# Loads of w_mod's units: from the sync engine's queue to ScalarE's own, one unit per round, two steps ahead of use

## The chip, the cores and the metric

The kernel runs on one core of a Trainium2 chip (trn2). The metric is the device time of one execution in microseconds (us), with all inputs in the chip's memory at the start and the output there at the end. The engines that matter here are PE (TensorE, matmuls), DVE (VectorE), ACT (ScalarE) and SP (the sync engine, which here only issues transfers). Each works through its own list in order; they meet through semaphores. 16 DMA engines move the data.

## What is computed

Two blocks on 256 tokens of width 2048, all in float32. The first has two layers of latent attention, a gated convolution, attention to a memory of 256 tokens, a gate and an output projection. The second is one layer with a Fourier mixer and an MLP of width 8192; both are modulated by six vectors of 2048 values that come from one vector `c` and a weight `w_mod` of 2048 x 12288:

```
# first block, for each of 2 layers
h = rmsnorm(x, pre_norm_g[l]);  z = h @ w_in[l]
q_lat, kv_lat, k_pe, gb, gc, xin, q_mem, gate = split_cols(z)
q = rmsnorm(q_lat) @ w_uq[l];  kv = rmsnorm(kv_lat) @ w_ukv[l]     # rope on parts of q and on k_pe
a_out = softmax(q k^T) v;  c_out = gb * conv(gc * xin)
m_out = memory attention of q_mem with rmsnorm(mem) @ w_mk[l], @ w_mv[l]
x = x + rmsnorm((concat(a_out, c_out, m_out) * silu(gate)) @ w_o[l], post_norm_g[l])
# second block
sh1, sc1, g1, sh2, sc2, g2 = split(silu(c) @ w_mod + b_mod, 6)
x = x + g1 * rms_norm(fft_mix(rms_norm(x) * (1 + sc1) + sh1) @ fnet_w_out)
x = x + g2 * rms_norm(relu(modulated(x, sh2, sc2) @ w_mlp_in)^2 @ w_mlp_out)
```

## The kernel before

**Steps.** The work is cut into 576 steps. Two steps use one weight unit of up to 1 MB (2048 columns on 128 partitions). A step's weights are split into a rounded high part (`whi`, made by ACT, line 383) and the rest (`wlo`, made by DVE in place of the raw weight, line 390), and PE multiplies both parts with a likewise split input (line 394). A full step keeps PE busy for about 2.72 us. Steps 0 to 143 are layer 1 of the first block, 144 to 287 layer 2, 288 to 319 the Fourier mixer's projection, 320 to 575 the MLP. In a layer the groups of steps are: memory keys and values, latents, `gc`, `uq`, `ukv` (steps of half the width), `xin`, `gb`, `qmem`, `gate`, `wo` (the last 32).

**Rings.** Four raw units (`raw`), four high halves (`whi`). In round s ACT and DVE first do the split for step s + 3 (`split_hi`, `split_lo`), then whatever else belongs to the round: softmax, the gate (xhalf, tanh, `Y`), squares, the reading of an accumulator that has ended. SP issues a weight unit when PE is through with the unit four before it (`load_unit`, line 357; semaphore `half_used`).

**w_mod.** The product silu(c) @ w_mod isn't done by PE but by DVE: `w_mod` is cut into 12 chunks of 1024 columns, each of 16 units of 128 rows (512 KB, one row of 4 KB per partition), 192 in all. DVE scales a unit and adds it to `modacc` (lines 1019 and 1022), in rounds that a planner picks (`MOD_AT`, two of them at most one step apart where DVE has room, none in rounds called `HEAVY`). After the 16th unit of a chunk PE adds up `modacc` over the partitions with 8 one-column matmuls (`mod_sums`), at the head of a step at least two after the last unit (`MOD_SUM`: steps 49, 82, 105, 126, 166, 204, 232, 255, 277, 308, 359, 421), and waits for that unit there (`mod_used`). The units of the fourth chunk end in step 124, its sum is in step 126; the eighth ends in step 253 and is summed in 255; the ninth ends in 275 and is summed in 277.

**The loads of these units.** They have three buffers (`modw`, `MRING`). Before, SP issues them between the weights: after the weight unit u come the mod units, if any, of steps 2u - 4 and 2u - 3 (`load_mods`, `MOD_LEAD` = 4; line 505), each behind a wait that DVE has used the unit three before it. ACT issues only a few transfers of its own, among them `rowb`, 1 MB that is spread from a row in memory to all partitions (line 692), and SP also the memory's tiles for the next layer (`memr`, line 508, behind a wait) and the gains.

Of the kernel before, what the change touches and what calls it, by code (L numbers as in the profile page):

```python
# [13 lines left out]
P = 128  # L14
# [3 lines left out]
KT = D // P  # L18
# [46 lines left out]
FN_H = DEPTH * LH  # L65
# [74 lines left out]

MCH = MODCOLS // 1024
MRING = 3
MOD_LEAD = 4
M3_BUSY = {q + PV_LAG for q in QK_AT}

HEAVY = ({21, 24, 26, 28, 30, 31, 32, 33, 39, 40, 41, 42, 44, 46, 48, 49, 51, 52, 54, 55, 56, 63} | set(range(64, 69)) | {72, 77, 84}
# [64 lines left out]
def build_program(nc, x, memt, positions, small, w_in, w_uq, w_ukv, w_mk, w_mv, w_o, post_g,  # L211
# [3 lines left out]
    with ctx:  # L215
# [277 lines left out]
        @block.sync  # L493
        def _(sp):
            mem_w = (w_mk, w_mv)

            def load_mods(step):

                for s in (step, step + 1):
                    if s in MOD_AT:  # L500
                        j = MOD_AT[s]
                        if j >= MRING:
                            sp.wait_ge(mod_used, j - MRING + 1)
                        k, c = j % KT, j // KT
                        sp.dma_start(modw[j % MRING][:, :], w_mod[k * P:(k + 1) * P, 1024 * c:1024 * (c + 1)]).then_inc(mod_in[j % MRING], 16)

            def load_mem(b):
                sp.dma_start(memr[:, b % 2, :, :], memt[4 * b:4 * b + 4].rearrange("k p n -> p k n")).then_inc(memr_in[b % 2], 16)

            def load_memx(b):  # L510
                sp.dma_start(memx[:, 4 * b:4 * b + 4, :], memt[4 * b:4 * b + 4].rearrange("k p n -> p k n")).then_inc(mem_in[b], 16)

            for i in range(2):
                sp.dma_start(memx[:, 2 * i:2 * i + 2, :], memt[2 * i:2 * i + 2].rearrange("k p n -> p k n")).then_inc((mem_first, mem_in[0])[i], 16)
                sp.dma_start(raw[0][:, 1024 * i:1024 * (i + 1)].rearrange("p (k n) -> p k n", k=2),
                             weight_rows(w_mk[0], 2 * i, 2, 0, 512)).then_inc((first_in, raw_in[0])[i], 16)
            for l in range(DEPTH):
                src = {"qlat": (w_in[l], C_Q), "kvlat": (w_in[l], C_KV), "gc": (w_in[l], C_GC), "uq": (w_uq[l], 0),
                       "ukv": (w_ukv[l], 0), "xin": (w_in[l], C_XIN), "gb": (w_in[l], C_GB), "qmem": (w_in[l], C_QM),
                       "gate": (w_in[l], C_GATE), "wo": (w_o[l], 0)}  # L520
                for g, (name, kind, width, units, nk) in enumerate(GROUPS):
                    for i in range(units):
                        at_unit = UNIT_AT[g] + i
                        u = l * LU + at_unit
                        if kind == "MEM":
                            if u:
                                load_unit(sp, u, slot(u, nk, width), weight_rows(mem_w[i % 2][l], i // 2 * nk, nk, 0, width))
                            if l == 0 and 1 <= i < 4:
                                load_memx(i)
                            if l == 0 and i == 3:  # L530
                                sp.dma_start(ident[:, :], consts).then_inc(ident_in, 16)
                                sp.dma_start(cv[:, 0:KT], cvec).then_inc(c_in, 16)
                                sp.dma_start(ropev[:, :], rope_c).then_inc(rope_in, 16)
                                sp.dma_start(pos[:, :], positions.partition_broadcast(P)).then_inc(rope_in, 16)
                                sp.dma_start(modT[:, :], bmod).then_inc(vec_in, 16)
                                sp.dma_start(ngs[:, :], ng2).then_inc(vec_in, 16)
                            if l == 0 and i == 4:
                                sp.dma_start(X[:, :, :], x.rearrange("(t p) d -> p t d", p=P)).then_inc(x_in, 16)
                            if l and at_unit in (2, 4):
                                b = at_unit // 2 + 1  # L540
                                sp.wait_ge(mem_lo, l * KT + 4 * (b - 1))
                                load_mem(b)
                        else:
                            w, c0 = src[name]
                            if name == "gate":
                                of = g - G_OF[name]
                                c0 = C_GATE + (2 * GATE_PART[of // 2] + of % 2 - of) * width
                            load_unit(sp, u, slot(u, nk, width),
                                      weight_rows(w, i * nk, nk, c0 + (g - G_OF[name]) * width, width))
                        load_mods(2 * u - MOD_LEAD)  # L550
                    if g == G_OF["wo"] - 1:

                        sp.wait_ge(o_out, l * NH + NH)
                        sp.wait_ge(conv_step, 12 * l + 12)
                        if l + 1 < DEPTH:
                            sp.dma_start(gs[:, :], small[l + 1]).then_inc(small_in, 16)
                        else:
                            sp.dma_start(cs[:, :, :], dft.rearrange("(t p) n -> p t n", p=P)).then_inc(dft_in, 16)
                        sp.dma_start(post[:, :], post_g[l:l + 1, :].partition_broadcast(P)).then_inc(post_in, 16)
                    if g == G_OF["wo"] + 1 and l + 1 < DEPTH:  # L560
                        sp.wait_ge(y_lo, l * 4 + 4)
                        load_mem(0)
                        load_mem(1)
            for i in range(4):
                u = FN_H // 2 + i
                load_unit(sp, u, slot(u, 4, 512), weight_rows(w_fnet, 4 * i, 4, 0, 512))
                load_mods(2 * u - MOD_LEAD)
            for n in range(1, 4):
                for i in range(4):
                    u = FN_H // 2 + 4 * n + i  # L570
                    load_unit(sp, u, slot(u, 4, 512), weight_rows(w_fnet, 4 * i, 4, 512 * n, 512))
                    load_mods(2 * u - MOD_LEAD)
            for q in range(4):
                for n in range(8):
                    for i in range(4):
                        u = ML_H // 2 + 32 * q + 4 * n + i
                        w = w_mlp_in[:, D * q:D * (q + 1)] if n < 4 else w_mlp_out[D * q:D * (q + 1), :]
                        load_unit(sp, u, slot(u, 4, 512), weight_rows(w, 4 * i, 4, 512 * (n % 4), 512))
                        load_mods(2 * u - MOD_LEAD)
            for i in range(2 * MT):  # L580
                sp.wait_ge(x_new, 10 + i + 1)
                t, c = i // 2, slice(i % 2 * (D // 2), (i % 2 + 1) * (D // 2))
                sp.dma_start(out[t * P:(t + 1) * P, c], X[:, t, c]).then_inc(stored, 16)
            sp.wait_ge(stored, 32 * MT)
# [42 lines left out]
        def _(act):  # L627
# [23 lines left out]
            def token_end(stage, t):  # L651

                if t == 0:
                    act.wait_ge(token_done, stage + 1)
                else:
                    act.wait_ge(half_used, BY_TOKEN[stage] + 8)

            def round_mem(l, f):
                if l == 0:
# [98 lines left out]
            for l in range(DEPTH):  # L758
                base = l * LH
                for s in range(LH):  # L760
                    if base + s + AHEAD < stage_end(base + s):
                        split_hi(act, base + s + AHEAD)
                    if l and s == 0:
                        ended(act, l - 1, NG - 1)
                    if l == 0 and s == 20:
# [112 lines left out]
            for s in range(32):  # L878
                if FN_H + s + AHEAD < ML_H:
                    split_hi(act, FN_H + s + AHEAD)  # L880
                if s and s % 8 == 0:
                    n = s // 8 - 1
                    act.wait_ge(half_used, FN_H + s)
                    row_squares([acc[n % 2][:, t * 512:(t + 1) * 512] for t in range(MT)], n)
                    act.wait_ge(row_sq, 2 * (4 * DEPTH + n) + 2)
                    act.sem_inc(acc_act, 1)
# [33 lines left out]
            for q in range(4):  # L920
                base = ML_H + 64 * q
                for s in range(64):
# [4 lines left out]
                        split_hi(act, base + s + AHEAD)  # L927
                    if more:
                        x2_round(s + AHEAD)
                    if s in (8, 16, 24, 32):  # L930
                        j = s // 8 - 1
                        act.wait_ge(half_used, base + s)
                        nc.scalar.activation(cross[:, :, :], banks[:, 4 * (j % 2):4 * (j % 2) + 4, SEQ:], ACT.Copy).then_inc(m_cross, 1)
                        act.wait_ge(m_sq, 4 * q + j + 1)
                        nc.scalar.activation(Yhi[:, 4 * j:4 * j + 4, :], sqr[:, :, :], ACT.Copy).then_inc(m_hi, 1)  # L935
# [792 lines left out]
```

## Time and profile before

| | us |
|---|---|
| median of three runs | 1729.94 |
| lowest and highest | 1727.78, 1731.48 |
| the profiled execution | 1728.09 |
| its span | 1725.9 |
| PE busy in it | 1691.7 |
| DVE busy | 1181.2 |
| ACT busy | 850.4 |

The span runs from the first to the last instruction; some 2 us of the execution lie outside it. Busy times are sums over the span, and PE's are modelled from a pipeline, so a busy PE need not be at its full speed; the granted clock tells that (1.00 is 2.4 GHz, 0.50 is 1.2 GHz).

### The profile page before, as it was taken

To read this page: it belongs to the slowest core of one execution; us is meant where nothing else is said; L and a number is where in the kernel's file an instruction comes from. 1 tells how busy PE (TensorE), PEld (TensorE's weight loads), DVE (VectorE), ACT (ScalarE), POOL (GpSimd) and SP (SyncE) were. 2 spreads that over 40 slices of the span, in tenths; PEclk is the share of its full clock that TensorE was granted. 3 is DMA by queue.
4 is the path that set the end of the run, shared out by engine and by line. 5 is a ranking of instruction groups with operands and counts; after the bars stand their busy time and mean duration, and the time that the engine had idled before them with its cause. 6 is when DMAs were issued, how large, how long until landed. Compare 5 with 4: busy or idle time off the path is not lost.

```text
span 1725.9 us, 22666 instructions
## 1 busy us (share of the span) xinstructions
PE 1691.7 (98%) x9156; PEld 1464.6 (85%) x9156; DVE 1181.2 (68%) x1278; ACT 850.4 (49%) x1187; POOL 19.4 (1%) x34
## 2 busy tenths in 40 slices
PE   7999999999999999999999989999999999999997
PEld 6899888878889988888898778888888888888886
DVE  6787757887867777787759567777555555455655
ACT  7557546444645654653454464433443344334442
POOL 0000000000100000000000000000000000000000
PEclk9999999999999999999999989999999999999999
DMA  8688667998668857697639548788655665665653
GB/s 300 213 288 300 205 202 251 323 344 296 240 203 288 287 192 260 220 340 295 242 135 343 197 154 284 262 289 278 182 190 191 185 187 195 218 184 184 194 195 122
DMA packets 217703, 408.16 MB, mean 236 GB/s; under 512 B 8928, under 2 KB 87040, under 8 KB 216832
## 3 DMA queue, kind: packets, MB, share of 16 engines
q1 hardware_dynamic: 217104, 404.58, 69.2%
q10 hardware_dynamic: 496, 2.14, 0.3%
q8 instruction: 73, 1.20, 0.3%
q14 instruction: 30, 0.25, 0.0%
HBM read 404.58 MB, written 2.11 MB: 236 GB/s over the span
## 4 chain that ended last, share of the span: by engine, by line
PE 91%; DVE 3%; DMA 3%; issue 2%; ACT 1%; POOL 0%; DVEq 0%; POOLq 0%; SPq 0%; ACTq 0%
PE banks L394 90%; DMA modw<-in_w_mod 2%; DVE modacc L1022 1%; DVE wlo L390 1%; DMA raw<-in_w_mv 1%; PE banks L1467 1%; PE banks L1430 0%; ACT whi L383 0%; DMA raw<-in_w_in 0%; DMA raw<-in_w_mk 0%; DVE otok L951 0%; PE banks L1438 0%; DVE X L991 0%; PE banks L1623 0%; ACT junk L636 0%
## 5 line engine op out<-in xcount | busy, mean ns | idle before, releaser
L390 DVE TENSOR_TENSOR wlo<-raw,whi 128x1024 fp32r<-128x1024 f32 (+3 forms) x563 | 666.0, 1189 | 416.7 <-ACT whi L383 414.5
L383 ACT ACTIVATE whi<-raw 128x1024 fp32r<-128x1024 f32 (+3 forms) x563 | 575.8, 1030 | 620.2 <-PE banks L394 585.3
L394 PE MATMUL banks<-H,whi 128*128 128x512 f32 x2048 | 734.3, 402 | 1.3 <-DVE H L951 1.2
L394 PE MATMUL banks<-H,wlo 128*128 128x256 f32 x2048 | 574.8, 281 | 0.0
L394 PEld LDWEIGHTS banks<-H,whi 128*128 128x128 f32 x2048 | 386.2, 189 | 93.3 <-DVE H L951 1.6
L394 PE MATMUL banks<-whi,Y 128*128 128x512 f32 x1472 | 458.4, 391 | 1.1 <-DVE wlo L390 1.1
L394 PEld LDWEIGHTS banks<-H,wlo 128*128 128x128 f32 x2048 | 388.2, 190 | 0.9
L394 PEld LDWEIGHTS banks<-whi,Y 128*128 128x128 f32 x1472 | 277.3, 188 | 60.4 <-DVE wlo L390 1.9
L394 PE MATMUL banks<-wlo,Y 128*128 128x512 f32 x768 | 299.6, 390 | 0.0
L1022 DVE SCALAR_TENSOR_TENSOR modacc<-modw,cv,modacc 128x1024 f32<-128x1024 f32 x180 | 230.1, 1278 | 17.5 <-DMA modw<-in_w_mod 17.4
L394 PEld LDWEIGHTS banks<-wlo,Y 128*128 128x128 f32 x768 | 144.6, 188 | 29.4
L394 PE MATMUL banks<-whi,H 128*128 128x512 f32 (+1 forms) x480 | 139.3, 370 | 0.0
L394 PEld LDWEIGHTS banks<-whi,H 128*128 128x128 f32 x480 | 87.6, 188 | 13.8
L394 PE MATMUL banks<-wlo,H 128*128 128x512 f32 (+1 forms) x256 | 94.5, 369 | 0.0
L394 PEld LDWEIGHTS banks<-wlo,H 128*128 128x128 f32 x256 | 48.1, 188 | 7.3
L798 ACT ACTIVATE prob<-banks,sc 128x256 f32<-128x256 f32 x48 | 22.4, 471 | 57.4 <-DVE sc L1187 57.4
L394 PE MATMUL banks<-memh,whi 128*128 128x256 f32 x128 | 37.8, 296 | 6.7 <-DVE wlo L951 6.6
L935 ACT ACTIVATE Y<-sqr 128x1024 fp32r<-128x1024 f32 x16 | 17.0, 1061 | 44.3 <-DVE sqr L1356 44.3
L394 PE MATMUL banks<-memh,wlo 128*128 128x256 f32 x128 | 37.0, 289 | 0.0
L394 PE MATMUL banks<-meml,whi 128*128 128x256 f32 x128 | 37.0, 289 | 0.0
L852 ACT ACTIVATE prob<-prob,sc 128x256 f32<-128x256 f32 x48 | 21.9, 503 | 22.4 <-DVE sc L1191 22.4
L951 DVE TENSOR_TENSOR Y<-sqr,Y 128x1024 fp32r<-128x1024 f32 x16 | 19.6, 1225 | 18.0 <-ACT Y L935 18.0
(202 smaller groups left out, 1338.7 us busy)
## 6 DMA issues: line engine op xcount, KB each, us to landing
modw<-in_w_mod SPq DMA_DIRECT2D x192, 512.0 KB, 6.5
raw<-in_w_in SPq DMA_DIRECT2D x72, 1024.0 KB, 5.4
raw<-in_w_mlp_in SPq DMA_DIRECT2D x64, 1024.0 KB, 5.5
raw<-in_w_mlp_out SPq DMA_DIRECT2D x64, 1024.0 KB, 5.0
raw<-in_w_o SPq DMA_DIRECT2D x32, 1024.0 KB, 6.8
raw<-in_w_fnet SPq DMA_DIRECT2D x16, 1024.0 KB, 6.1
raw<-in_w_mv SPq DMA_DIRECT2D x8, 1024.0 KB, 6.0
raw<-in_w_mk SPq DMA_DIRECT2D x7, 1024.0 KB, 6.8
```

Source lines behind the costliest of these rows:

```text
L383: nc.scalar.activation(hi_part(step, n), raw[u % RAW][:, (step % 2) * n:(step % 2) * n + n], ACT.Copy).then_inc(hi_ready, 1)
L390: nc.vector.tensor_tensor(wlo[u % RAW][:, part], raw[u % RAW][:, part], hi_part(step, n).bitcast(F32), ALU.subtract).then_inc(lo_ready, 1)
L394: return nc.tensor.matmul(o, a, b, start=start, stop=stop, skip_group_check=True)
L798: w = nc.scalar.activation(prob[:, b, t, :], M[b][:, t * SEQ:(t + 1) * SEQ], ACT.Exp, scale=scale, bias=sc[:, NM + 2 * b + t:NM + 2 * b + ...
L852: w = nc.scalar.activation(prob[:, b, t, :], prob[:, b, t, :], ACT.Copy, scale=sc[:, RINV + 2 * b + t:RINV + 2 * b + t + 1])
L935: nc.scalar.activation(Yhi[:, 4 * j:4 * j + 4, :], sqr[:, :, :], ACT.Copy).then_inc(m_hi, 1)
L951: return nc.vector.tensor_tensor(o, a, b, op)
L1022: nc.vector.scalar_tensor_tensor(modacc[:, :], modw[j % MRING][:, :], co, modacc[:, :], ALU.mult, ALU.add).then_inc(mod_used, 1)
L1467: i = nc.tensor.transpose(M[2][:, kt * SEQ + t * P:kt * SEQ + (t + 1) * P], prob[:, b, t, kt * P:(kt + 1) * P], ident[:, :])
```

## The change

SP no longer loads mod units. ACT does, on its own queue: in round s, right after `split_hi` for step s + 3, it issues the unit of step s + 2, if that step has one, behind the same wait for a free buffer. The planner's tables, the buffers, DVE's and PE's lists and the bytes moved are unchanged.

```
-MOD_LEAD = 4
+MOD_LEAD = 2
...
-            def load_mods(step):
-
-                for s in (step, step + 1):
-                    if s in MOD_AT:
-                        j = MOD_AT[s]
-                        if j >= MRING:
-                            sp.wait_ge(mod_used, j - MRING + 1)
-                        k, c = j % KT, j // KT
-                        sp.dma_start(modw[j % MRING][:, :], w_mod[k * P:(k + 1) * P, 1024 * c:1024 * (c + 1)]).then_inc(mod_in[j % MRING], 16)
-
...
-                        load_mods(2 * u - MOD_LEAD)
...
+            def load_mod(step):
+
+                if step + MOD_LEAD in MOD_AT:
+                    j = MOD_AT[step + MOD_LEAD]
+                    if j >= MRING:
+                        act.wait_ge(mod_used, j - MRING + 1)
+                    k, c = j % KT, j // KT
+                    act.dma_start(modw[j % MRING][:, :], w_mod[k * P:(k + 1) * P, 1024 * c:1024 * (c + 1)]).then_inc(mod_in[j % MRING], 16)
...
                     if base + s + AHEAD < stage_end(base + s):
                         split_hi(act, base + s + AHEAD)
+                    load_mod(base + s)
...
                 if FN_H + s + AHEAD < ML_H:
                     split_hi(act, FN_H + s + AHEAD)
+                load_mod(FN_H + s)
...
                     if more:
                         x2_round(s + AHEAD)
+                    load_mod(base + s)
```

The first place is `wo` in layer 1, steps 118 to 128 (360 to 390 us in the trace). SP's list there before; `raw_51` to `raw_54` are the four raw buffers, `modw_112` to `modw_114` the three of the mod units:

```order
135 L357 DMA raw_52<-in_w_o 128x4x512 [waits half_used]
136 L505 DMA modw_113<-in_w_mod 128x1024 [waits mod_used]
137 L505 DMA modw_114<-in_w_mod 128x1024 [waits mod_used]
138 L357 DMA raw_53<-in_w_o 128x4x512 [waits half_used]
139 L505 DMA modw_112<-in_w_mod 128x1024 [waits mod_used]
140 L357 DMA raw_54<-in_w_o 128x4x512 [waits half_used]
141 L505 DMA modw_113<-in_w_mod 128x1024 [waits mod_used]
142 L505 DMA modw_114<-in_w_mod 128x1024 [waits mod_used]
143 L508 DMA memr<-in_memt 128x4x256 [waits y_lo]
144 L508 DMA memr<-in_memt 128x4x256
145 L357 DMA raw_51<-in_w_o 128x4x512 [waits half_used]
146 L505 DMA modw_112<-in_w_mod 128x1024 [waits mod_used]
```

The last row is the chunk's 16th unit. SP's list there now (line numbers have moved by 10):

```order
77 L357 DMA raw_52<-in_w_o 128x4x512 [waits half_used]
78 L357 DMA raw_53<-in_w_o 128x4x512 [waits half_used]
79 L357 DMA raw_54<-in_w_o 128x4x512 [waits half_used]
80 L498 DMA memr<-in_memt 128x4x256 [waits y_lo]
81 L498 DMA memr<-in_memt 128x4x256
82 L357 DMA raw_51<-in_w_o 128x4x512 [waits half_used]
```

The weights and the memory's tiles are left, with no wait for `mod_used` between them. ACT's list there before:

```order
296 L383 ACTIVATE whi_62<-raw_52 128x1024 [waits half_used,raw_in1]
297 L636 ACTIVATE junk,sc<-banks 128x512 [waits half_used]
298 L636 ACTIVATE junk,sc<-banks 128x512
299 L383 ACTIVATE whi_59<-raw_53 128x1024 [waits row_sq,half_used,raw_in2]
300 L383 ACTIVATE whi_60<-raw_53 128x1024 [waits half_used,raw_in2]
```

And now:

```order
357 L383 ACTIVATE whi_62<-raw_52 128x1024 [waits half_used,raw_in1]
358 L651 DMA modw_113<-in_w_mod 128x1024 [waits mod_used]
359 L622 ACTIVATE junk,sc<-banks 128x512 [waits half_used]
360 L622 ACTIVATE junk,sc<-banks 128x512
361 L383 ACTIVATE whi_59<-raw_53 128x1024 [waits row_sq,half_used,raw_in2]
362 L651 DMA modw_114<-in_w_mod 128x1024 [waits mod_used]
363 L383 ACTIVATE whi_60<-raw_53 128x1024 [waits half_used,raw_in2]
364 L651 DMA modw_112<-in_w_mod 128x1024 [waits mod_used]
```

A load with its wait now stands behind each `whi` of such a round and ahead of the next; row 364 is the 16th unit.

The second place is the end of `ukv` in layer 2 (571 to 584 us), where the units grow from 512 KB to 1 MB. SP's list before:

```order
210 L357 DMA raw_53<-in_w_ukv 128x2x512 [waits half_used]
211 L357 DMA raw_54<-in_w_ukv 128x2x512 [waits half_used]
212 L505 DMA modw_114<-in_w_mod 128x1024 [waits mod_used]
213 L357 DMA raw_51<-in_w_in 128x8x256 [waits half_used]
214 L505 DMA modw_112<-in_w_mod 128x1024 [waits mod_used]
215 L357 DMA raw_52<-in_w_in 128x8x256 [waits half_used]
```

ACT's list there now:

```order
524 L383 ACTIVATE whi_59<-raw_53 128x512 [waits half_used,raw_in2]
525 L383 ACTIVATE whi_60<-raw_53 128x512 [waits half_used,raw_in2]
526 L719 ACTIVATE V<-banks 128x2x256 [waits half_used]
527 L724 ACTIVATE kn<-banks 128x512
528 L383 ACTIVATE whi_61<-raw_54 128x512 [waits half_used,raw_in3]
529 L651 DMA modw_112<-in_w_mod 128x1024 [waits mod_used]
530 L383 ACTIVATE whi_62<-raw_54 128x512 [waits half_used,raw_in3]
531 L719 ACTIVATE V<-banks 128x2x256 [waits half_used]
532 L724 ACTIVATE kn<-banks 128x512
533 L383 ACTIVATE whi_59<-raw_51 128x1024 [waits half_used,raw_in0]
```

The mod unit of row 214, which stood behind the weight unit of row 213 in one queue, is now row 529 of ACT's list, on another queue than that weight unit.

## Rows read from the trace of the kernel before

**Rows 1.** The page's busy time of each engine: us, share of the span, instructions

```profile
PE 1691.7 (98%) x9156; PEld 1464.6 (85%) x9156; DVE 1181.2 (68%) x1278; ACT 850.4 (49%) x1187; POOL 19.4 (1%) x34
```

**Rows 2.** Waits: engine, line, releaser, us, times, longest; the last from 760:845 alone

```profile
PE banks L394 <- DVE modacc L1022: 5.5, 4, 2.2
...
DVE modacc L1022 <- DMA modw<-in_w_mod: 17.4, 17, 3.1
...
DVE modacc L1022 <- DMA modw<-in_w_mod: 4.6, 3, 3.0
```

**Rows 3.** Timeline of PE: start, us, instruction, idle time before it and releaser

```profile
389.44 1.22 PE L394 MATMUL banks<-ones,modacc 128*128 128x1 f32 x6 [2.21 <-DVE modacc L1022]
...
776.13 1.92 PE L394 MATMUL banks<-ones,modacc 128*128 128x1 f32 x16 [2.02 <-DVE modacc L1022]
...
840.34 1.92 PE L394 MATMUL banks<-ones,modacc 128*128 128x1 f32 x16 [0.55 <-DVE modacc L1022]
```

**Rows 4.** Busy time in stretches, granted clock, share of the DMA engines, GB/s

```profile
386.00:398.00 12.00, 9.79 (x38) 8.21 (x37) 3.72 (x4) 2.48 (x3) 0.00 (x0) 0.72 0.75 284
774.00:784.00 10.00, 7.98 (x41) 6.99 (x41) 5.24 (x7) 3.73 (x5) 0.00 (x0) 0.83 0.29 100
...
372.00:390.00 18.00, 15.79 (x72) 12.87 (x70) 14.90 (x15) 7.49 (x11) 0.00 (x0) 0.99 1.05 390
```

**Rows 5.** Timeline of DVE, 371 to 392 us

```profile
377.83 1.28 DVE L1022 SCALAR_TENSOR_TENSOR modacc<-modw,cv,modacc 128x1024 f32<-128x1024 f32 x1
...
382.49 1.28 DVE L1022 SCALAR_TENSOR_TENSOR modacc<-modw,cv,modacc 128x1024 f32<-128x1024 f32 x1
383.69 1.22 DVE L390 TENSOR_TENSOR wlo<-raw,whi 128x1024 fp32r<-128x1024 f32 x1
388.01 1.28 DVE L1022 SCALAR_TENSOR_TENSOR modacc<-modw,cv,modacc 128x1024 f32<-128x1024 f32 x1 [3.10 <-DMA modw<-in_w_mod]
```

**Rows 6.** Timeline of SP's issues, 355 to 392 us; two in one row hold a wait

```profile
364.01 3.79 SPq L505 DMA_DIRECT2D modw<-in_w_mod  x2
367.85 0.43 SPq L357 DMA_DIRECT2D raw<-in_w_o  x1
...
374.85 0.98 SPq L508 DMA_DIRECT2D memr<-in_memt  x2
376.39 0.37 SPq L357 DMA_DIRECT2D raw<-in_w_o  x1
379.14 0.34 SPq L505 DMA_DIRECT2D modw<-in_w_mod  x1
```

**Rows 7.** Timeline of ACT and DVE ahead of the gap at 776.13

```profile
765.03 1.06 ACT L846 ACTIVATE Y<-gate 128x1024 fp32r<-128x1024 f32 x1 [3.62 <-DVE gate L1070]
...
767.07 1.23 DVE L390 TENSOR_TENSOR wlo<-raw,whi 128x1024 fp32r<-128x1024 f32 x1 [2.07 <-ACT whi L383]
```

**Rows 8.** SP's issues of mod units (ns), their landing; rowb's landing, the last number

```profile
L505 SPq DMA_DIRECT2D modw<-in_w_mod x192: 327/449/2242, 62.9 to 1193.4; - x192
...
DMA to landing us min/median/max: 3.7/6.5/11.3
...
rowb<-mod_rows ACTq DMA_DIRECT2D x1, 1024.0 KB, 9.8
```

**Rows 9.** SP's waits for a mod buffer: us in total, times, longest

```profile
SPq L505 <- DVE modacc L1022: 129.6, 76, 5.1
```

**Rows 10.** Timeline of ACT, 806.5 to 808.5 us: an issue beside an ACTIVATE

```profile
807.25 1.06 ACT L383 ACTIVATE whi<-raw 128x1024 fp32r<-128x1024 f32 x1 [0.51 <-PE banks L394]
807.27 0.38 ACTq L692 DMA_DIRECT2D rowb<-mod_rows  x1
```

**Rows 11.** The chain that ended last, 560 to 600 us: start, us, what

```profile
574.30 6.03 DMA raw<-in_w_in
...
582.85 0.49 ACT kn L729
583.34 0.04 issue
583.39 16.65 PE banks L394 x97
```

More of the change, by code:

```diff
@@ L566, in _ @@
                 load_unit(sp, u, slot(u, 4, 512), weight_rows(w_fnet, 4 * i, 4, 0, 512))
-                load_mods(2 * u - MOD_LEAD)
             for n in range(1, 4):
@@ L571, in _ @@
                     load_unit(sp, u, slot(u, 4, 512), weight_rows(w_fnet, 4 * i, 4, 512 * n, 512))
-                    load_mods(2 * u - MOD_LEAD)
             for q in range(4):
@@ L578, in _ @@
                         load_unit(sp, u, slot(u, 4, 512), weight_rows(w, 4 * i, 4, 512 * (n % 4), 512))
-                        load_mods(2 * u - MOD_LEAD)
             for i in range(2 * MT):
```

## Prediction

> **What bounds the kernel now.** The page comes first: PE, the TensorE engine, is busy 1691.7 of 1725.9 us; ACT works 850.4 us and DVE 1181.2 [rows 1]. So the end moves only with PE's gaps and its clock; the reader should look for gaps that come from w_mod's units. PE's own waits give four behind the accumulation of these units, 5.5 us together [rows 2]. The timeline places three of them, each in front of a sum over `modacc`: 2.21 us at 389.44, 2.02 at 776.13 and 0.55 at 840.34 [rows 3]; the rest, 0.7 us, stands in front of the sum of the chunk before 389, near 327. The stretches show a second price. In the 12 us around the second gap the granted clock is 0.72 of full, in the 10 us around the third 0.83 [rows 4]. At half speed a share of (1 - clock) of the stretch is lost: 12 x 0.28 = 3.4 us and 10 x 0.17 = 1.7 us. The most there is to win is thus 5.5 + 3.4 + 1.7 = 10.6 us, 0.6%.
>
> The two large gaps differ in cause. At 389.44 it is a transfer. DVE ends its work at 383.69 + 1.22 = 384.9 and sits idle 3.10 us until the 16th unit of the fourth chunk lands at 388.0 [rows 5]. That unit was issued at 379.14, the moment DVE had freed its buffer (377.83 + 1.28 = 379.1) [rows 5, 6]. Ahead of it in the same queue stood the weight unit of 376.39 and the two memory loads of 374.85 [rows 6], 2 MB, while the DMA engines were at 1.05 of their time and 390 GB/s [rows 4]: 2.1 MB / 390 GB/s is 5.4 us. At 776.13 no transfer is late: ACT waits 3.62 us for DVE's gate product before `Y`, DVE then waits 2.07 us for ACT's next `whi`, and from 767.07 on no transfer is named as DVE's releaser up to the sum at 776.13 [rows 3, 7].
>
> **What the change does, part by part.** *Time of issue.* Before, SP issues the units of two steps behind a weight unit; after, ACT issues one unit in each round, right behind its `whi` of three steps on. Both wait for the same thing, a free one of three buffers. The unit of 379.14 must still wait for 379.1, so it is issued no earlier. Units of odd steps can go up to one step (2.72 us) later; ready units have gone before they were needed in all but 17 of 192 cases, 17.4 us of DVE time in all [rows 2], and the dense stretches are held by the buffers anyway.
>
> *The queue.* What changes is what stands ahead of it: on ACT's queue only mod units, so it shares the DMA engines with the weights in place of following them. How fast is half a megabyte then? The smallest landing is 3.7 us [rows 8]; less 0.52 MB / 390 GB/s = 1.3 us that leaves 2.4 us fixed. The nearest row for two queues under load is `rowb`, 1 MB on ACT's queue beside a full SP queue: 9.8 us to landing [rows 8], so (9.8 - 2.4) / 1.05 MB = 7.1 us per MB. For the unit: 2.4 + 0.52 x 7.1 = 6.1 us. Ends: 3.7 us (nothing beside it) and 8.85 us (as now). I take 6.1, since it was measured between these two queues. It lands at 385.2; DVE starts 0.3 us late, ends at 386.5, and PE, which ends its half-step at about 387.2, does not wait. Late next is DVE itself, with 0.7 us to spare. The gap of 2.2 us goes and with it the clock's 3.4 us: **5.6 us**.
>
> The Trainium skill, page "DMA: Bandwidth & Descriptors", section "Queues, rings and completion order", says each DMA engine goes round the queues that have work, packet by packet. By an even share the unit would take 2.4 + 2 x 1.3 = 5.1 us and land at 384.2, and the sum would stay at 5.6. `rowb`'s 9.8 us [rows 8] is slower than an even share, so I keep the row's figure.
>
> *Weights off the hook.* SP now sits 129.6 us in 76 waits for a mod buffer [rows 9], and weights queue behind it: the unit of 367.85 follows such a wait directly [rows 6]. These waits go. In the stretch 760 to 845 DVE waits three times, 4.6 us, for mod units [rows 2], so the 0.55 us gap at 840.34 has cover and falls away: **0.5 us** (ends 0 and 0.55). The gaps at 327.19 and 776.13 stay, as DVE has no transfer to wait for.
>
> *ACT's own cost.* It gets 192 issues. On SP one takes 0.33 to 2.24 us, median 0.45 [rows 8]; ACT's one neighbour, the issue of `rowb` at 807.27, took 0.38 us and ran from 0.02 us after the start of a `whi` of 1.06 us [rows 10], thus under it. Cost on the path: 0 (all hidden) to 0.4 us in each place where PE waits for ACT. Worse could be the wait for the buffer, up to 5.1 us each [rows 9], now on ACT with its `whi` of the next round, the gate's and softmax's ACTIVATEs and the accumulator's read queued behind it. In a dense stretch it ends when DVE ends a unit; DVE then has a `wlo` of 1.22 us and a unit of 1.20 us (382.49 to 383.69) of its own [rows 5] before it needs the next `whi`, which takes ACT 0.4 + 1.06 us. Taken: 0.
>
> *Weights beside mod units.* The price is at the end of `ukv` in the second layer. The weight unit of 574.30 lands after 6.03 us, ACT reads the accumulator behind it until 583.34, and PE goes on at 583.39 [rows 11]. The mod unit that SP issues next (the second place in the section on the change) follows it now; afterwards it goes beside it and can take up to its own 1.3 us from it. Ends 0 and 1.3; there PE pays one for one. No row is nearer to one end; I take the middle, **-0.7 us**. At the same place of the first layer the chain of waits holds no weight transfer; I take 0.
>
> **Sum:** 5.6 + 0.5 - 0.7 = 5.4 us off. The profiled execution took 1728.09 us (span 1725.9), so 1722.7 us for a like one. Three runs have the median 1729.94, 1.9 us above it: the forecast is **1724.5 us**, -0.3%.
>
> **The rivals.** *The transfer is no earlier (0.30).* The stretch 372 to 390 has the DMA engines at 1.05 [rows 4]; if the unit still lands after 387 - 1.3 = 386, PE waits at least part of 2.2 us and the clock falls. For it: the load is the same, in bytes and place, and the issue time is set by the buffer. Against it: `rowb` did get through beside the SP queue. Time: 1729.9, with the small terms cancelling, 1728 to 1732. The Trainium skill states a rule that ends here: page "DMA: Bandwidth & Descriptors", section "Issuing engines are not separate DMA queues": starting DMAs on several engines only saves the sequencer's time. By that rule the kernel stays at 1729.9; [rows 8] do not speak against it for the sum of bytes, but speak for a changed order among them.
>
> *Weights starve (0.18), the slower side.* Mod units take their share from the weight units wherever the DMA engines are full. Place: 575 to 590, where ACT waits for `raw` and PE for ACT. It decides once two units in a row come late by 1.3 us each: PE then stands over 2 us, and after the gaps of 2.0 and 2.2 us the clock fell (1.7 and 3.4 us [rows 3, 4]). With the old gap uncured that is 2.6 + 2.5 = 5 us: 1735, from 1733 up; with it cured the two cancel near 1730. For it: this is the one place where a weight transfer is on the chain of waits. Against it: the mod units are held to three buffers, and PE's wait there is short today.
>
> *All of it (in the forecast's case).* If less lateness also shortens DVE's chain before 776, up to 10.6 us go: 1719.3.
>
> **How the numbers follow.** Forecast 0.52 (1719.5 to 1726.4), no earlier transfer 0.30 (1728 to 1732), starved weights 0.18 (1733 and up). A measurement of this kernel can tell about 0.2%, 3.5 us, from no change. So faster 0.52, same 0.30, slower 0.18. The range 1719.5 to 1732.5 leaves out most of the last case and a little below. The forecast's own range is 1719.5 to 1726.4.
>
> **What would show it.** Right: no gap before the sum near 389, granted clock 1.00 there, the unit's landing some 6 us, gaps at 327 and 776 as before, no row of SP waiting for `modacc`, ACT's issues lying under `whi`. Wrong: ACT waiting for `modacc` with DVE waiting for `whi` behind it; a landing over 7 us near 385; PE's start after `ukv` later than 9.1 us behind the issue of that weight unit (574.30 to 583.39 now); a clock under 1.00 in a stretch that has 1.00 now.

## The result, and the profile after

| | before | after |
|---|---|---|
| median in this comparison, us | 1731.05 | 1735.47 |
| lowest and highest of 20 runs each | 1727.17, 1734.34 | 1731.39, 1741.0 |
| span of the profiled execution | 1725.9 | 1733.1 |

The ratio is 1.0024 with the interval [1.0015, 1.0033]: the change makes the kernel slower, by 0.24% or about 4.2 us. The forecast was 1724.5 us, and its range ended at 1732.5.

On the page of the changed kernel, PE, DVE and ACT do what they did [rows 1]; PE's busy time is longer by 6 us although its list is the same; its mean granted clock over the span was 0.990 in place of 0.993. Mod units (one unit of `w_mod`) now have a queue of their own, q10. The rows are busy time, bytes by queue (MB, share of 16 engines), and loads with the median us to landing:

```profile
PE 1697.7 (98%) x9156; PEld 1468.3 (85%) x9156; DVE 1180.9 (68%) x1278; ACT 850.2 (49%) x1187; POOL 21.5 (1%) x34
...
q1 hardware_dynamic: 189456, 303.90, 53.6%
q10 hardware_dynamic: 28144, 102.82, 16.7%
...
modw<-in_w_mod ACTq DMA_DIRECT2D x192, 512.0 KB, 5.3
raw<-in_w_in SPq DMA_DIRECT2D x72, 1024.0 KB, 7.1
...
raw<-in_w_o SPq DMA_DIRECT2D x32, 1024.0 KB, 7.5
```

The same loads on the page of the kernel before:

```profile
modw<-in_w_mod SPq DMA_DIRECT2D x192, 512.0 KB, 6.5
raw<-in_w_in SPq DMA_DIRECT2D x72, 1024.0 KB, 5.4
...
raw<-in_w_o SPq DMA_DIRECT2D x32, 1024.0 KB, 6.8
```

This is the change in three rows of medians: a mod unit lands 1.2 us sooner, a unit of `w_in` 1.7 us and one of `w_o` 0.7 us later. The waits of the changed kernel (us in total, times, longest) say who pays:

```profile
ACT whi L383 <- DMA raw<-in_w_in: 27.9, 13, 5.2
ACT whi L383 <- DMA raw<-in_w_o: 25.0, 10, 6.1
ACT whi L383 <- DVE modacc L1020: 13.1, 6, 3.1
DVE modacc L1020 <- DMA modw<-in_w_mod: 8.8, 9, 1.8
...
PE banks L394 <- DVE modacc L1020: 5.9, 4, 2.8
...
PE banks L394 <- DVE wlo L390: 2.5, 4, 0.8
```

Before, the first two were:

```profile
ACT whi L383 <- DMA raw<-in_w_o: 19.6, 9, 4.3
...
ACT whi L383 <- DMA raw<-in_w_in: 8.2, 6, 3.1
```

DVE's waits for mod units were halved, as wanted (17.4 us before [rows 2]), while ACT's for weights went from 27.8 to 52.9 us. PE's four gaps in front of sums did not shrink as a whole: 5.9 us for 5.5 [rows 2]. PE's timeline, against [rows 3]:

```profile
329.55 2.02 PE L394 MATMUL banks<-ones,modacc 128*128 128x1 f32 x16 [0.70 <-DVE modacc L1020]
...
392.12 1.92 PE L394 MATMUL banks<-ones,modacc 128*128 128x1 f32 x16 [1.09 <-DVE modacc L1020]
...
777.19 2.46 PE L394 MATMUL banks<-ones,modacc 128*128 128x1 f32 x16 [2.83 <-DVE modacc L1020]
...
843.96 1.92 PE L394 MATMUL banks<-ones,modacc 128*128 128x1 f32 x16 [1.31 <-DVE modacc L1020]
```

The gap at 389 was halved (2.21 to 1.09 us), those at 777 and 844 grew (2.02 to 2.83, 0.55 to 1.31). The stretches round them (the third number from the end of a row is the granted clock), against [rows 4]:

```profile
325.00:339.00 14.00, 13.30 (x74) 11.61 (x73) 9.83 (x12) 4.29 (x5) 0.00 (x0) 0.88 0.88 309
386.00:402.00 16.00, 14.91 (x75) 12.34 (x74) 10.35 (x12) 6.31 (x9) 0.00 (x0) 1.00 0.89 309
772.00:788.00 16.00, 13.17 (x60) 11.29 (x59) 9.01 (x11) 5.13 (x6) 0.00 (x0) 0.79 0.44 152
838.00:854.00 16.00, 14.69 (x66) 11.99 (x65) 9.38 (x9) 4.97 (x5) 0.00 (x0) 0.89 0.55 192
```

The same stretches of the kernel before:

```profile
325.00:339.00 14.00, 13.29 (x82) 11.57 (x82) 9.29 (x11) 5.82 (x7) 0.00 (x0) 1.00 1.02 375
386.00:402.00 16.00, 13.79 (x55) 11.54 (x54) 6.25 (x7) 4.80 (x7) 0.00 (x0) 0.79 0.61 220
772.00:788.00 16.00, 13.98 (x70) 11.89 (x69) 10.33 (x12) 5.77 (x7) 0.00 (x0) 0.89 0.56 206
838.00:854.00 16.00, 15.45 (x77) 12.79 (x77) 9.36 (x10) 6.61 (x11) 0.00 (x0) 1.00 0.55 191
```

So the two traces differ by a half-speed stretch at 329 behind an equal gap, one fewer at 392, a longer one at 777 and a new one at 844. Besides, PE has a new place where it waits. In steps 32 and 33 (the first of `uq`, each 2.8 us of work) it stood for `wlo`. The chain that ended last, 85 to 112 us, of the changed kernel:

```profile
89.49 9.55 DMA raw<-in_w_in
...
99.06 1.07 ACT whi L383
...
101.29 1.28 DVE modacc L1020
102.57 1.57 DVE qll L1128 x4
104.14 1.14 DVE wlo L390
```

Before, there is nothing but PE in this stretch; the same weight unit, issued at 89.24, landed after 5.9 us. The mod unit of step 29, which followed it in SP's queue, now goes beside it on ACT's, and the one before that (issued at 87.82, landed at 93.23) does so in part: the weight unit took 3.6 us longer. The two steps took 3.7 and 3.9 us in place of 2.8 each: 1.9 us.

Durations of the steps concerned, from one step's last matmul to the next's, in the profiled executions, in us (the matmuls of a sum's step alone take 4.6; the gap ahead of a sum is in brackets):

| kernel | 32 + 33 | sum at 327 | sum at 389 | sum at 777 | sum at 844 |
|---|---|---|---|---|---|
| before | 5.6 | 5.6 (0.71) | 10.2 (2.21) | 8.4 (2.02) | 5.3 (0.55) |
| after | 7.5 | 7.1 (0.70) | 5.9 (1.09) | 10.6 (2.83) | 7.7 (1.31) |

The differences in this table add up to 3.7 us, while the two spans differ by 7.2. The traced execution of the kernel before was a quick one (1728.09 us, with a median of 1731.05), that of the changed kernel lay at its median. Of the other 3.5 us, 0.5 stand in step 320 and 0.4 in step 177; the rest is spread in smaller parts. So two traces alone don't say where the loss of 4.2 us lies; the experiments have to.

### The profile page after: what moved, and what is told of

It reads as the page before. It is cut to its first block, busy times and chain, and to the rows that moved or that the text cites. A ratio compares the mean times of both kernels' runs of the same rounds, so it can differ in the third digit from the quotient of the medians.

```text
span 1733.1 us, 22666 instructions
## 1 busy us (share of the span) xinstructions
PE 1697.7 (98%) x9156; PEld 1468.3 (85%) x9156; DVE 1180.9 (68%) x1278; ACT 850.2 (49%) x1187; POOL 21.5 (1%) x34
## 4 chain that ended last, share of the span: by engine, by line
PE 89%; DMA 4%; DVE 3%; issue 2%; ACT 1%; POOL 0%; DVEq 0%; POOLq 0%; ACTq 0%; SPq 0%
PE banks L394 88%; DMA raw<-in_w_o 2%; DMA raw<-in_w_in 1%; DVE modacc L1020 1%; DMA raw<-in_w_mv 1%; DVE wlo L390 1%; PE banks L1465 1%; ACT whi L383 1%; PE banks L1428 0%; DMA modw<-in_w_mod 0%; DVE otok L949 0%; DMA raw<-in_w_mk 0%; DVE qll L1128 0%; DVE X L989 0%; PE banks L1621 0%
## 5 line engine op out<-in xcount | busy, mean ns | idle before, releaser
L394 PEld LDWEIGHTS banks<-whi,H 128*128 128x128 f32 x480 | 87.7, 188 | 13.7
L394 PEld LDWEIGHTS banks<-memh,whi 128*128 128x128 f32 x128 | 25.7, 201 | 7.5 <-issue 7.4
```

What stands on the lines that cost most here:

```text
L394: return nc.tensor.matmul(o, a, b, start=start, stop=stop, skip_group_check=True)
```

## Experiments

The rival explanations of the loss. *A, shared DMA engines:* on a queue of its own the mod unit takes time from weight units that were ahead of it, and `whi`, `wlo` and PE pay where a weight is nearly late. *B, ACT blocked:* ACT now stands in front of a busy mod buffer (13.1 us in the row above) with its next `whi` behind it. *C, scatter:* clock and gaps differ from one execution to the next. With 20 executions of each kernel the loss itself is clear of this (the interval starts at 1.0015); a single gap in a single trace is not. *D, later issue:* units of odd steps are asked for later.

### ACT's waits alone

Both queues as before; ACT only waits where the changed kernel issues.

```
+                if step + MOD_LEAD in MOD_AT:
+                    j = MOD_AT[step + MOD_LEAD]
+                    if j >= MRING:
+                        act.wait_ge(mod_used, j - MRING + 1)
```

> SP loads the mod units in the old order; ACT issues none of them, but waits for the same free buffers at the same places as in the changed kernel. Theory A (weights starve: mod units on a queue of their own take DMA time from the weight units): the weights again come first, so this runs like the kernel before, 0 to +1.5 us, with no gap in front of the steps near 101 and 104 us and weight units landing as before (5.4 us median for w_in). Theory B (ACT stands at the buffer wait and its whi comes late): +4 us like the changed kernel, with ACT waiting some 13 us for modacc and the gaps near 101, 389, 776 and 843 us.

Measured: 1731.77 us beside 1731.91, ratio 0.9996 [0.9982, 1.001]. Steps 32 and 33 took 2.8 us each. ACT's waits for mod buffers ahead of a `whi`:

```profile
ACT whi L384 <- DVE modacc L1033: 14.7, 7, 3.6
```

It stood for buffers even longer than in the changed kernel (14.7 us) and lost nothing. B falls as the cause of a loss of 0.24%, since the interval ends at 1.001; the prediction's 0 for these waits holds within it.

### Later issue on SP's queue

Of the two units behind a weight, the second waits until PE is two steps ahead of its use; all stays on SP's queue.

```
+                        if s > step:
+                            sp.wait_ge(half_used, s - 2)
```

> The mod units stay on SP's queue, but the second of a pair is held back until PE begins the step two ahead of its use, as the changed kernel has it. Theory A: one queue keeps the weights in order, so within 1.5 us of the kernel before; the weight units near 89 us land after 6 to 7 us. Theory C (the later issue, two steps ahead for every unit, is what costs): +3 to +5 us, with DVE waiting longer for mod units.

Measured: 1732.71 us beside 1731.91, ratio 1.0005 [0.9992, 1.0019]; steps 32 and 33 at 2.8 us, the gap at 389 at 1.96. By the middle value D is a fifth of the loss. The interval holds zero, but also more than half of the loss, so the time alone doesn't exclude D; that steps 32 and 33 lost nothing does, for that place.

### A quarter of the bytes, on either queue

Only 256 of the 1024 columns of each mod unit are loaded, the rest of the buffer is zero; the sums over the other columns are left out in this way. The zeros are written once, at the start; everything else, the number of issues too, stays.

```
-                    act.dma_start(modw[j % MRING][:, :], w_mod[..., 1024 * c:1024 * (c + 1)])
+                    act.dma_start(modw[j % MRING][:, 0:256], w_mod[..., 1024 * c:1024 * c + 256])
```

On ACT's queue:

> The changed kernel, but each mod unit brings only 256 of its 1024 columns (the rest of the buffers holds zeros, so the modulation vectors are incomplete). Same issues and waits on ACT, a quarter of the bytes. Theory A: the loss against the same kernel with SP's queue (the next run) is gone, within 1.5 us. Theory B: the loss of about 4 us stays. Both: faster than with all bytes, as the gaps made by late transfers go (the one near 389 us, 5.6 us with its clock).

On SP's:

> The kernel before with the same quarter loads (256 of 1024 columns of each mod unit, zeros in the rest). Against the kernel before, all theories: -5 to -7 us, since the transfer behind the gap near 389 us is no longer late; the gaps near 327 and 776 us, which no transfer makes, stay.

Measured: 1724.59 us on ACT's queue (ratio 0.9956 [0.9941, 0.9971]), 1725.17 on SP's (0.9966 [0.9953, 0.9978]), beside 1731.91. With 75 MB less (192 x 0.39) no difference between the queues is left that these runs can tell. In both traces PE had no gap in front of the sums at 389 and 844, and the gaps at 327 and 777 stayed (0.71 and 1.92 us). The landings with ACT's queue:

```profile
raw<-in_w_in SPq DMA_DIRECT2D x72, 1024.0 KB, 5.7
...
raw<-in_w_o SPq DMA_DIRECT2D x32, 1024.0 KB, 5.2
modw<-in_w_mod ACTq DMA_DIRECT2D x192, 128.0 KB, 3.7
```

A `w_in` unit needs 5.7 us beside the small mod units and 7.1 beside the full ones. The loss hangs on bytes, not on ACT's instructions: A.

### The early units back on SP's queue

In the changed kernel the first 12 mod units (used in steps 18 to 37) are issued by SP again.

```
+ON_SP = set(range(0, 12))
...
+                        load_mods(2 * u - 4)
...
-                if step + MOD_LEAD in MOD_AT:
+                if step + MOD_LEAD in MOD_AT and MOD_AT[step + MOD_LEAD] not in ON_SP:
```

> The changed kernel with the first 12 units of w_mod (used in steps 18 to 37, 70 to 120 us) back on the sync engine's queue, the other 180 on ScalarE's. If the price at 101 to 108 us comes from the unit of step 29 (89.7 to 98.8 us) sharing the DMA engines with the w_in unit issued at 89.49, that weight unit lands within 6 to 7 us again (9.5 in the changed kernel), PE has no wait for wlo at 101 to 108 us, and the kernel takes 1.9 us less than the changed one: 1733.6 beside a before of 1731, ratio 1.0013. If the price comes from something else that ACT's queue brings along, the two steps stay at 3.7 and 3.9 us and the time at 1735.5.

Measured: 1733.88 us beside 1732.83, ratio 1.0014 [1.0002, 1.0026]; A expected 1.0013. Steps 32 and 33 are at 2.8 us again. ACT's wait ahead of them is 2.09 us in this kernel's timeline; it was 5.24 us in the changed one:

```profile
95.45 1.06 ACT L384 ACTIVATE whi<-raw 128x1024 fp32r<-128x1024 f32 x1 [2.09 <-DMA raw<-in_w_in]
```

The intervals of 1.0014 and 1.0024 overlap, so the 1.7 us between them is no firm figure. Nor is the stall's size: in the traces of the two other kernels that leave these units on ACT's queue with all their bytes (the late units back, and both cures, below) it is 0.3 and 0.5 us in place of 1.9. That it goes with these units is clear: no trace with them on SP's queue has it. The late units are still on ACT's queue here, and the sum at 777 again has a long gap (2.80 us, a step of 10.8), while the one at 844 has 0.52 us in place of 1.31 (a step of 6.5).

### The late units back on SP's queue, and both

`ON_SP` holds the units of the eighth and ninth chunk, 112 to 143:

> The changed kernel with the units of the eighth and ninth chunk (used in steps 232 to 275, 705 to 842 us) back on the sync engine's queue. If the longer gaps in front of the two sums (2.8 in place of 2.0 us at 777, 1.3 in place of 0.55 at 844) are due to weight units that land late (13.0 and 13.7 us in place of 10.2 and 10.9), the gaps are 2.0 and 0.6 us again and the two steps take 4.6 us less than in the changed kernel: 1731 beside a before of 1731, ratio 1.000; less if the clock falls as before by chance. If the gaps are only scatter of one execution, the time stays at 1735.5.

and, in a second kernel, these and the first 12:

> Both undone: the units of the first 12 and of the eighth and ninth chunk on the sync engine's queue, 148 on ScalarE's, among them the fourth chunk, whose sum gained 4.3 us. If the places add up, it is 6.5 us below the changed kernel: 1729 beside a before of 1731, ratio 0.9985 to 0.999. If the loss is spread over all places, it lies at 1732 to 1734.

Measured: 1733.01 us, ratio 0.9999 [0.9988, 1.001], and 1730.4 us, ratio 0.9991 [0.9979, 1.0002], beside 1732.83. Against the 1.0024 of the changed kernel the late units are worth 0.25% (4.3 us; expected 4.6), the early ones 0.10% (1.7 us; 1.9), both 0.33% (5.7 us; 6.5): within the intervals they add up. These kernels undo the queue and the time of issue at once. The gap at 844 went to 0.46 us in the first and to none in the second; as the kernel with the early units back had 0.52 us there with its late units on ACT's queue, the 1.31 us of the changed kernel are in part scatter. Scatter of the same kind stands in the second kernel's trace at a sum that has no gap in any other (step 359): 0.54 us, and a step of 6.9 us in place of 4.6. At 777 the expectation missed: the first kernel's trace has a gap of 2.98 us, though its mod units are on SP's queue, the second's 1.92. DVE's timeline in the first shows why:

```profile
771.57 1.22 DVE L391 TENSOR_TENSOR wlo<-raw,whi 128x1024 fp32r<-128x1024 f32 x1
773.76 1.28 DVE L1031 SCALAR_TENSOR_TENSOR modacc<-modw,cv,modacc 128x1024 f32<-128x1024 f32 x1 [0.97 <-DMA modw<-in_w_mod]
```

and in the changed kernel:

```profile
771.94 1.28 DVE L1020 SCALAR_TENSOR_TENSOR modacc<-modw,cv,modacc 128x1024 f32<-128x1024 f32 x1
773.13 0.68 DVE L949 TENSOR_TENSOR gate<-banks,xhalf 128x512 f32<-128x512 f32 x1
774.62 1.23 DVE L390 TENSOR_TENSOR wlo<-raw,whi 128x1024 fp32r<-128x1024 f32 x1 [0.81 <-ACT whi L383]
```

with ACT's timeline behind it:

```profile
773.53 1.06 ACT L383 ACTIVATE whi<-raw 128x1024 fp32r<-128x1024 f32 x1 [4.80 <-DMA raw<-in_w_o]
```

DVE's work ahead of this sum has no slack, so whatever comes late adds to the gap: on SP's queue the mod unit (0.97 us, and the gap 2.98 for 2.02), on ACT's the weight unit (0.81 us, and the gap 2.83). In the trace of before the mod unit landed at 771.75 and was used at 771.77: just in time. The same loads must all land there, and the queue settles which is last. The memory's tiles later (below), on SP's queue, show the mod unit late by 0.9 us and a gap of 2.95; of the seven traces with full units on SP's queue these two have it late by that much, while in both traces with them on ACT's queue the weight unit is late, by 0.81 and 0.79 us.

### One chunk on ACT's queue

The kernel before, with the fourth chunk's 16 units alone issued by ACT two steps ahead.

```
+ON_ACT = set(range(48, 64))
...
-                    if s in MOD_AT:
+                    if s in MOD_AT and MOD_AT[s] not in ON_ACT:
...
+                if MOD_AT.get(step + 2) in ON_ACT:
```

> The kernel before with only the fourth chunk's 16 units (used in steps 105 to 124, 330 to 390 us) issued by ScalarE two steps ahead. If the forecast's term for the gap at 389 was right by itself and only the weights elsewhere made the loss, the step of that sum takes 5.9 us in place of 10.2 (4.6 if the gap is gone altogether) and the kernel 4.3 to 5.6 us less than before: 1725.5 to 1727 beside 1731, ratio 0.997. If the gain there is given back within the same stretch, the ratio is 1.000.

Measured: 1730.38 us beside 1732.83, ratio 0.9983 [0.9972, 0.9994], 2.9 us (1.0 to 4.8 by the interval) where 4.3 to 5.6 had been expected. The forecast's central term exists; its middle value is about half of 5.6. The sum's row and its stretch:

```profile
390.23 1.92 PE L395 MATMUL banks<-ones,modacc 128*128 128x1 f32 x16 [0.79 <-DVE modacc L1032]
```

```profile
386.00:402.00 16.00, 15.21 (x69) 12.39 (x68) 9.56 (x11) 5.28 (x8) 0.00 (x0) 0.89 0.77 273
```

The gap shrank from 2.21 to 0.79 us, but the clock fell all the same.

### Other cures: the memory's tiles later, the sums later

The two `memr` loads that stood ahead of the 16th unit [rows 6] are issued one group of `wo` later, all on SP's queue:

```
-                    if g == G_OF["wo"] + 1 and l + 1 < DEPTH:
+                    if g == G_OF["wo"] + 2 and l + 1 < DEPTH:
```

> The kernel before with one edit: the first two loads of the memory's tiles for layer 2 go out one wo group (four weight units) later, behind the unit that made the gap near 389 us. Theory of the forecast's price (the gap is a transfer held up by what stands ahead of it in the queue, and brings the clock down): the gap near 389 us goes, -5.6 us with the clock's share, -2.2 if the clock falls anyway. Rival (DMA engines are full there in any order): the gap stays, 0 to -1 us.

Measured: 1728.44 us beside 1732.21, ratio 0.9975 [0.9961, 0.9988]. The unit landed 5.8 us after its issue (8.85 before), and the sum followed without a gap, in 4.6 us: the step is 5.6 us shorter than before. The whole kernel gained 4.3 us.

```profile
390.68 1.84 PE L394 MATMUL banks<-ones,modacc 128*128 128x1 f32 x16
...
774.99 3.33 PE L394 MATMUL banks<-ones,modacc 128*128 128x1 f32 x16 [2.95 <-DVE modacc L1022]
```

The second row is the sum at 777 again: this trace has the long gap there, so its own span gained less than the step did.

The four sums with a gap one step later, on SP's queue:

```
+MOD_SUM = {s + (c in (2, 3, 7, 8)): c for s, c in MOD_SUM.items()}
```

> The kernel before with one edit: PE adds up the chunks 3, 4, 8 and 9 one step (2.72 us) later. If the four gaps (0.7, 2.2, 2.0, 0.55 us) are PE arriving too early for DVE's last unit and the clock's fall follows from them, all but a part of the one at 389 go: -8 to -10.6 us. If the clock falls with the sums themselves: -5.5 us. If the units of the next chunk come late for it in turn: less, and DVE waits for PE's sum.

Measured: 1718.18 us, ratio 0.9922 [0.9907, 0.9938]: 13.5 us less, the best kernel of this study. PE has no wait for `modacc` left, and all four stretches are at full clock, two of them here:

```profile
386.00:402.00 16.00, 15.86 (x79) 13.15 (x78) 11.63 (x13) 7.40 (x10) 0.00 (x0) 1.00 0.95 339
772.00:788.00 16.00, 16.00 (x74) 13.20 (x74) 11.01 (x16) 6.98 (x8) 0.00 (x0) 1.00 0.90 328
```

Both edits, once on SP's queue and once in the changed kernel:

> The two edits of the runs before together, with the mod units on SP's queue: no gap in front of a sum, granted clock 1.00 from 100 to 860 us, -10 to -10.6 us against the kernel before.

> The changed kernel with the same two edits. Theory A: sums find their units, so of the change's loss only the steps stay at which PE waits for late weights (1.9 us near 101 to 108 us, 0.2 to 0.4 us in other places): 2 to 3 us slower than the run before this one, -7 to -8 us against the kernel before. Theory B: the loss of 4 us or more stays beside the run before this one.

Measured: 1718.24 us (0.9925 [0.9911, 0.994]) on SP's and 1721.0 (0.9934 [0.9918, 0.995]) on ACT's queue, beside 1732.21. With the sums later the memory's tiles gained nothing more that could be told. What ACT's queue costs is 0.09% (1.5 us) by the ratios and 2.8 us by the medians, in place of 4.2; with six executions each, neither is clear of zero. So a part of the change's loss goes through the sums, but how large a part isn't shown. Steps 32 and 33 still lost 0.5 us in the trace on ACT's queue. The expectation of no gap in front of a sum missed once: on SP's queue the sum of the eighth chunk had one of 1.11 us, with the granted clock at 1.00 in the 16 us from 764 and in those from 772.

## Why the prediction was wrong, point by point

*The four gaps as the prize: right, but too small.* "The most there is to win is thus 5.5 + 3.4 + 1.7 = 10.6 us"; moving the sums won 13.5. The trace of before was a kind one: behind the 0.71 us gap at 327 the clock stayed at 1.00, while of the ten other kernels that kept the sum in its place (the changed one and nine experiments) nine show it fall: its step took 7.0 to 7.3 us in place of 5.6.

*The gap at 776, "stay, as DVE has no transfer to wait for": wrong.* No transfer was named as a releaser there, but a mod unit had landed just 0.02 us before its use and a weight unit had no slack. The step took 10.6 and 10.8 us in the two traces with these units on ACT's queue, and 8.4 in that of before.

*The transfer at 389: right in kind.* It no longer waits behind 2 MB, and landed after 6.9 us; 6.1 had been taken, from `rowb`. But "it is issued no earlier" missed that it could be issued later. It was issued 7.3 us ahead of PE's end of step 125, not 8.1, since DVE freed the buffer that much later: four units earlier it had waited for one (the row below). So 2.0 us won in flight and 0.85 lost at issue leave a gap of 1.09, not none.

```profile
377.81 1.28 DVE L1020 SCALAR_TENSOR_TENSOR modacc<-modw,cv,modacc 128x1024 f32<-128x1024 f32 x1 [0.80 <-DMA modw<-in_w_mod]
```

*The clock's 3.4 us with it: right by luck in this trace, wrong as a term.* The price was taken to go in step with the gap. Gaps of 0.8 to 1.1 us in front of this sum had a clock of 1.00 (after), 0.89 (fourth chunk alone, late units back) and 0.79 (early units back, both back) in 16 us; 2.21 us before had 0.79. At 844, 0.19 us (later issue) had 0.89. In no trace did the clock fall behind a sum without a gap: those steps took 4.6 us (3.4 and 5.1 for the sums of steps 49 and 232) in all fourteen traces, within 0.25 us (one with a gap of 0.14 us among them is 0.3 us longer). But the gap doesn't stand alone: 1.8 us of one-column matmuls, the sum, follow it. The gaps of 0.63 and 0.79 us in steps 32 and 33, with full matmuls behind them, left the clock at 1.00 (changed kernel):

```profile
98.00:112.00 14.00, 12.58 (x73) 10.86 (x72) 10.91 (x12) 9.88 (x19) 4.21 (x2) 1.00 0.97 316
```

The term of 5.6 us measured 2.9 us when it was made alone. Where the gap was removed entirely, by the memory's loads, the kernel gained 4.3 us, and the step 5.6 in its trace.

*The hook at 840, "0.5 us (ends 0 and 0.55)": wrong in sign, the step that failed with the next one.* The term looked only at mod units coming sooner. In the changed kernel the chain that ended last runs through a weight there:

```profile
812.57 13.72 DMA raw<-in_w_o
...
826.31 1.07 ACT whi L383
```

The chain of before has mod units there:

```profile
805.07 11.07 DMA modw<-in_w_mod
...
819.81 7.42 DMA modw<-in_w_mod
```

So the mod units had been last, as the term had it; now it is a `w_o` unit in flight for 13.7 us (10.9 before). `rowb` and four mod units were in flight on ACT's queue during this time, and DVE's work up to the sum moved with the weight. The gap became 1.31 us, the step 7.7 for 5.3. In the kernel with the early units back the same weight unit took 12.7 us and the gap was 0.52. Undoing the late chunks gave 4.3 us back; in its trace 2.4 us of that stand in this step, and the one at 777 gained nothing.

*Weights beside mod units, "the middle, -0.7 us": the failed term.* It was priced at one place, 574, because only there a weight transfer stood on the chain that ended last. That place was nearly free: after 6.21 us in flight in place of 6.03, PE went on 0.2 us later. The price fell on weights with little slack that were on no chain before: the unit of 89.24 had landed 0.3 us ahead of its `whi`, those of `w_o` at 770 and 820 with none. The sum should have taken every weight unit with little slack. The upper end of 1.3 us for one of them was too low as well, since more than one mod unit can go beside a weight unit: those of 89.24, 760 and 812 took 3.6, 2.8 and 2.8 us longer. Measured instead of 0.7: about 1.7 us early and 4.3 late.

*ACT's own cost, 0: right.* An issue took 0.33 to 0.40 us and ran beside ACTIVATEs; the buffer waits of 13.1 us cost nothing that ACT's waits alone could tell from zero. One row of each kind in the changed kernel:

```profile
757.83 1.06 ACT L383 ACTIVATE whi<-raw 128x1024 fp32r<-128x1024 f32 x1 [1.23 <-DMA raw<-in_w_in]
757.85 0.33 ACTq L651 DMA_DIRECT2D modw<-in_w_mod  x1
```

*The rivals.* "Weights starve" was the right mechanism, with its 1735 and a chance of 0.18; its place (575 to 590) was wrong, and so was its condition, two late units in a row: one late unit sufficed where DVE had no slack before a sum. *No earlier transfer* was wrong: the unit was faster. The Trainium skill, page "DMA: Bandwidth & Descriptors", section "Issuing engines are not separate DMA queues", says the choice of issuing engine saves sequencer time and no more. With a quarter of the bytes that held here (1724.6 and 1725.2 us); with all of them the order among the transfers changed, the median landings by 0.7 to 1.7 us, and the kernel by 0.24%, so the measurement decides against the rule for this load.

*The account.* The fourth chunk alone brings -2.9 us, the early units +1.7 and the late ones +4.3: +3.1 of the measured +4.2 [2.6 to 5.7]. What is left, 1.1 us, lies within the intervals. The steps in the traces of all kernels that kept the sums and full mod units agree in direction, with much scatter (us; the column says on which queue the units of that place were; the kernel with the memory's tiles later is left out at 389, those with later sums are in the first row too):

| steps | on SP's queue | on ACT's queue | difference of the means |
|---|---|---|---|
| 32 + 33 | 5.65 in all nine | 7.5, 5.9, 6.1 | +0.9 |
| sum at 389 | 10.2, 10.3, 10.0 | 5.9, 8.7, 7.5, 8.5, 7.2 | -2.6 |
| sum at 777 | 8.4, 8.5, 8.3, 11.0, 10.8, 9.9, 8.2 | 10.6, 10.8 | +1.4 |
| sum at 844 | 5.3, 6.8, 6.3, 4.8, 5.3, 4.6, 5.3 | 7.7, 6.5 | +1.6 |

These means add up to +1.3 us, so of the measured +4.2 the traces place no more than that at the four places; where the rest is lost stays open, as does how much of the late part is gap and how much clock.

## What to carry to other kernels

When loads move to a queue of their own, list the slack of every transfer that they overtake, not only of those on the chain that ended last; under full DMA engines what one kind of load won here (1.2 us in the median) the other paid (1.7). A small gap of the bounding engine is to be removed entirely, as halving it may leave the clock's share in place. And where a consumer's position is only a number in a table, moving the consumer one step is worth trying before its producer is sped up: here it won 13.5 us, and the earlier landing at 389 2.9.

## What was not expected of the hardware

The length of a short gap alone doesn't settle whether the clock falls: 0.7 to 0.9 us of idle PE at 327 was followed by a granted clock of 1.00 over 14 us in two of eleven traces and by 0.88 in nine. In the two the sum began at 327.2 us, in the nine at 327.8 to 329.6, so the moment may matter; no run varied it alone. After such a fall the sum's step was 1.5 us longer, twice the gap itself. Mod units were issued in at most 0.40 us each on ACT's queue and in up to 2.24 us on SP's [rows 8].
